# The lanes' turn every four blocks of the receptance and value tiles, in place of every eight

## What is computed

```python
r, k, v, xw, xa, xg = split_cols(rwkv_p, (RWKV_DIM, RWKV_DIM, RWKV_DIM, DECAY_LORA, AAA_LORA, GATE_LORA))
w_log = -jax.nn.softplus(-(rwkv_w0 + jnp.tanh(xw) @ rwkv_w2)) - 0.5
decay = jnp.exp(-jnp.exp(w_log.astype(jnp.float32)))
a = jax.nn.sigmoid(rwkv_a0 + xa @ rwkv_a2)
g = jax.nn.sigmoid(xg) @ rwkv_g2
kk = l2_normalize(hs(k * rwkv_k_k))
k = k * (1.0 + (a - 1.0) * rwkv_k_a)
y = rwkv7_recurrence(r_h, hs(decay), k_h, v_h, -kk, kk * a_h)
y = head_norm(y, rwkv_gn_w, rwkv_gn_b, RWKV_GN_EPS)
bonus = jnp.sum(r_h * k_h * rwkv_r_k, axis=-1, keepdims=True) * v_h
o_rwkv = ((y + bonus.reshape(B, S, RWKV_DIM)) * g).astype(x.dtype)
```

## Time and profile before

| | us |
|---|---|
| median of 3 runs | 3484.59 (3483.98 to 3485.78) |
| the profiled execution, own time | 3487.36 |
| its span, first to last instruction | 3485.6 |
| PE busy in the span | 3373.1 |
| DVE busy in the span | 2252.5 |
| the recurrence with `out_half`'s first tiles, from the trace | 276 (1158 to 1434) |

### The profile page before, as it was taken

How to read it: one execution, slowest core, us unless ns; L and a number is a source line. 1 busy time by engine, 2 the same in 40 slices (tenths; PEclk the granted TensorE clock), 3 DMA queues, 4 the chain that set the end, 5 groups by cost and what they waited for, 6 DMA issues and landing times.

```text
span 3485.6 us, 68747 instructions
## 1 busy us (share of the span) xinstructions
PE 3373.1 (97%) x30086; PEld 3319.7 (95%) x30086; DVE 2252.5 (65%) x3653; ACT 1620.8 (46%) x2339; POOL 56.6 (2%) x78
## 2 busy tenths in 40 slices
PE   7999999999998999999999999998999999999997
PEld 7999999999998888899999999998998999999997
DVE  5656655556676688696666655687546976666455
ACT  5544444444455534364444444464443644444443
POOL 0000000000000000000000000001000000000000
PEclk9999999999999999999999999999999999999998
DMA  6455555555564322255555666542543465555663
GB/s 230 163 176 176 174 176 185 175 180 176 176 197 134 106 89 86 94 171 197 194 194 194 195 191 191 188 151 82 166 147 127 158 199 194 194 194 191 194 198 127
DMA packets 162494, 586.38 MB, mean 168 GB/s; under 512 B 18128, under 2 KB 18128, under 8 KB 161936
## 3 DMA queue, kind: packets, MB, share of 16 engines
q1 hardware_dynamic: 160560, 574.01, 50.4%
q0 software_dynamic: 1632, 7.96, 0.8%
HBM read 579.80 MB, written 2.10 MB: 167 GB/s over the span
## 4 chain that ended last, share of the span: by engine, by line
PE 53%; DVE 8%; ACT 1%; issue 0%; POOL 0%; ACTq 0%; DVEq 0%; POOLq 0%
PE bank L2082 16%; PE bank L2084 16%; PE bank L2083 16%; DVE pairs L2871 2%; PE bank L2295 1%; PE bank L2282 1%; DVE xs L2987 1%; DVE xs L2985 0%; PE bank L2097 0%; PE bank L2099 0%; PE bank L2098 0%; ACT pairs L2548 0%; DVE xr L2955 0%; DVE xr L2875 0%; DVE xs L2901 0%
## 5 line engine op out<-in xcount | busy, mean ns | idle before, releaser
L2082 PE MATMUL bank<-xr,pairs 128*128 128x256 f32 (+1 forms) x5888 | 1660.9, 282 | 35.2 <-DVE pairs L2871 27.3
L2083 PE MATMUL bank<-xr,pairs 128*128 128x256 f32 (+1 forms) x5888 | 1640.3, 279 | 0.0
L2084 PE MATMUL bank<-xr,pairs 128*128 128x256 f32 (+1 forms) x5888 | 1640.2, 279 | 0.0
L2548 ACT ACTIVATE pairs<-raw 128x1024 fp32r<-128x1024 f32 (+1 forms) x1106 | 1143.4, 1043 | 981.3 <-PE bank L2084 791.7
L2871 DVE TENSOR_TENSOR pairs<-raw,pairs 128x1024 fp32r<-128x1024 f32 (+1 forms) x1106 | 1306.3, 1200 | 383.2 <-ACT pairs L2548 380.1
L2082 PEld LDWEIGHTS bank<-xr,pairs 128*128 128x128 f32 x5888 | 1115.7, 189 | 45.9 <-DVE pairs L2871 30.1
L2083 PEld LDWEIGHTS bank<-xr,pairs 128*128 128x128 f32 x5888 | 1113.9, 189 | 1.3
L2084 PEld LDWEIGHTS bank<-xr,pairs 128*128 128x128 f32 x5888 | 1113.3, 189 | 0.0
L2082 PE MATMUL bank<-parts,pairs 128*128 128x256 f32 x1792 | 496.5, 277 | 0.4 <-DVE parts L2875 0.4
L2084 PE MATMUL bank<-parts,pairs 128*128 128x256 f32 x1792 | 495.0, 276 | 0.0
L2083 PE MATMUL bank<-parts,pairs 128*128 128x256 f32 x1792 | 495.0, 276 | 0.0
(11 more groups left out here) (601 smaller groups left out, 3069.3 us busy)
## 6 DMA issues: line engine op xcount, KB each, us to landing
raw<-in_w_in SPq DMA_DIRECT2D x176, 512.0 KB, 4.5
raw<-in_gate SPq DMA_DIRECT2D x176, 512.0 KB, 5.5
raw<-in_val SPq DMA_DIRECT2D x176, 512.0 KB, 4.4
raw<-in_down SPq DMA_DIRECT2D x160, 512.0 KB, 4.4
raw<-in_l_w_in SPq DMA_DIRECT2D x144, 512.0 KB, 4.0
raw<-in_w_out SPq DMA_DIRECT2D x64, 512.0 KB, 4.8
raw<-in_l_w_out SPq DMA_DIRECT2D x64, 512.0 KB, 3.9
raw<-in_v_in SPq DMA_DIRECT2D x48, 512.0 KB, 5.3
```

The lines of the kernel that those rows point to most:

```text
L2082: mm(o, wh[:, q, :], rh[:, k, :], start=begin and q == 0, stop=False)
L2083: mm(o, wh[:, q, :], rl[:, k, :], start=False, stop=False)
L2084: last = mm(o, wl[:, q, :], rh[:, k, :], start=False, stop=end and q == c - 1)
L2548: e.activation(pair_of(n)[0], v3(raw_of(n), widths[n] // slices[n]), ACT.Copy).then_inc(*hi_made(n))
```

## The change

The two calls that issue the column matmuls of the receptance and the value tile pass `step` 4:

```diff
             p2 = v3(j.rv.view, 2)
-            col_tile(p2[:, 0, :], W(16 + c), X2, last.at, j.rv)
-            j.m = col_tile(p2[:, 1, :], W(24 + c), X2, last.at, j.rv)
+            col_tile(p2[:, 0, :], W(16 + c), X2, last.at, j.rv, 4)
+            j.m = col_tile(p2[:, 1, :], W(24 + c), X2, last.at, j.rv, 4)
             j.set = get(sets)
```

## The result

The change made the kernel slower, by more than was forecast:

| | before | after |
|---|---|---|
| median, us | 3484.73 (3483.98 to 3485.78, 4 runs) | 3528.64 (3527.20 to 3530.83, 4 runs) |
| the profiled execution, own time | 3487.36 | 3529.16 |
| its span | 3485.6 | 3527.4 |
| the recurrence, first `lora` matmul to last output matmul (L2397) | 275.3 | 316.6 |
| of it idle on PE, as shown | 11.0 | 29.0 |

A forecast was written before the change was run, and what follows sets the result against it. PE, busy 97% of the span, was taken as the bound. Bursts +8.4, bare stretches -7.8 and late preparation +25.8 sum to +26.4, cut for overlap to +22: 3506.6 us, range 3484 to 3526.

The forecast's parts named there:

- more bursts: Small matmuls among column matmuls: 73 groups in place of 38, each costing PE 0.24 us beyond its work, +8.4 us.
- shorter bare stretches: Two stretches without column matmuls: 20 turns left in place of 32, 3.9 us saved in each, -7.8 us.
- late preparation: At bonus matmul L2327 and at L2362: PE waits for VectorE's preparation, with column-matmul cover halved, +25.8 us.
- discount for overlap: Over the recurrence: VectorE catches up while PE waits, so the summed +26.4 was cut to +22 us.
- clock: Matmuls behind PE's long waits might run at 1.2 GHz, about 1.7 us lost each; left out of the sum.
- A slower PE also shortens the next wait, so I leave it out of the sum: Behind long PE waits: slow matmuls shorten the following wait, so their cost got no term, only a rival.
- rival 3: Behind most long waits the clock falls, six times 1.7 to 2.3 us on top: about +34, 3519 us; 16%.
- I take the middle, +22: Over the recurrence: chosen between the full sum, +26.4, and +18 at the ratio of the first cycle's walk.
- a walk over one cycle: First cycle followed on the clock: +6.0 us, where the terms' share would be 8.7.
- the price of 1.0 us a turn: In the new bare stretches: 20 turns at 1.0 us each, about 20 us a stretch, 5 of them lost.
- Rivals 1 and 2: Better-mixed lanes, bonus waits under about 1 us: 3475 us, 9%; 1.45 us waits cancelling bare-stretch savings: 3485 us, 13%.

The follow-up runs named there:

- value only: Kernel before with four-block turns for the value tile alone, the receptance tile keeping eight; 3494.41 us, ratio 1.0026.
- the filler kernel: Changed kernel with ten filler matmuls on constants between preparation steps PE waits for ahead of the bonus, c = 0, 1, 2, 5, 6; 3524.22 us, ratio 1.0111.
- two turns at once: Changed kernel's number of turns, taken two at a time every eight blocks instead of one every four; 3533.57 us, ratio 1.0138.

## Why the prediction was wrong, and what in it was right

The direction and the mechanism were right; the forecast of 3506.6 was 22 us short, and the time lies 2.6 us above the range. In the predicted order:

| term | predicted | measured | from |
|---|---|---|---|
| more bursts | 35 x 0.24 = +8.4 | some +14, or 0.4 each | what the other rows leave over |
| shorter bare stretches | -7.8 | about -6.2 | 72.8 to 44.3 us, less 22.3 of lane work moved out |
| late preparation | +25.8 | +23.7 | PE's idle time outside the bare stretches, 2.8 to 26.5 |
| discount for overlap | -4.4 | none | |
| clock | left out | +6.2 in column matmuls, some +3 to 4 in small ones | matmuls behind the waits |
| sum | +22 | +41.2 | |

The lane work moved out is an estimate: each matmul at the mean distance between starts that its kind has in the kernel before. The first row is a remainder and holds whatever else is not in the others; value only gave the same 0.4 for a burst.

**The step that failed first is "A slower PE also shortens the next wait, so I leave it out of the sum".** The clock was the largest term that was mis-sized: put at nothing, it measured some 9 to 10 us. It came as rival 3 had it ("falls at most of the long waits"), with 16%. The earlier trace rows had shown it for a wait of 3.06 us, and five of the forecast's own waits were as long or longer. The reason for leaving it out holds in part only: the filler kernel got 4.4 us back net of its own matmuls. The other reason, the bare stretches at 1.00, came from gaps of 1.3 us at most and says nothing of a gap of 3. The Trainium skill (TensorE: Matmul & The Clock Gate, "HAM oscillation — how this bites in real kernels") says that repeated idle time between groups of matmuls costs the clock again and again; the trace agrees, with 0.90 and 0.93 over the stretches with long waits and 1.00 over the bare ones with short ones.

**The second is "I take the middle, +22".** From a walk over one cycle that gave 6.0 for 8.7 I concluded that the terms overlap, and cut a sum of 26.4. The walk held the same assumption as the sum: that PE, once released, runs at full pace. It did not. With the full sum the forecast would have been 3511, which is still 18 short.

**The bursts**: 0.24 us was read where two lanes' steps stand together with 24 column matmuls behind the earlier trace rows. One lane's step with 12 behind costs 0.29 by the rows above, and about 0.4 is left for each over the region, which makes this term 5 to 6 us too small.

**The waits** were walked well one by one, and their mechanism was the predicted one, down to the third mask ahead of L3171. Predicted for c = 0 to 2: 2.1, 4.7, 3.6; measured 2.6, 4.9, 2.9. (The terms written out for c = 1 give 4.5, not 4.7: 1191.9 and 11.8 make 1203.7.) In front of L2362: 3.6 for c = 3, and most of 5.5 for c = 4, where 3.06 and 3.71 were measured; c = 5 2.5 against 3.1, c = 6 3.35 against 2.0. These waits are some 22 us where 25.8 were forecast. The wait of c = 7 (1.45 before), which was to stay, is gone. New was a wait of 2.7 us of `out_half`'s first column matmul (at 1388.92) for a low part, L2875, where before had 0.4 us; the walk did not contain it.

**The bare stretches** came out near the forecast: their idle time fell from 8.2 to 2.5 us, and the price of 1.0 us a turn was close (22.0 and 22.3 us for 20 turns and the burst ahead of them, 1.06 each).

With these put right: 22 + 4.4 (no discount) - 2.1 (waits) + 9.7 (clock) + 1.6 (bare stretches) + 5.6 (bursts, the remainder) = 41.2.

**Rivals 1 and 2** fell at the point that the prediction named: the bonus waits are not under 1 us. The Trainium skill (Perfetto Trace Analysis, "Optimization Strategy") holds that interleaving regimes with different bound engines may gain; the gain was about 6 us here, in the bare stretches, and the costs beside it some 47.

**Still open**: how much of the +41.2 the clock would keep if all waits were filled (the filler covered five lanes of eight, and not L2362); how the remainder of some 14 us divides between the bursts and the pace of small matmuls; and why a turn in a bare stretch costs 1.0 to 1.1 us whatever the mix. An order in which VectorE's low parts give way to a late preparation was not tried.

## What to carry to other kernels

Before making a side stream take turns more often, look up the chain that it starts with, on whatever engines it runs, and ask how many microseconds of the main engine's work lie between its issue and its first use: here 10.8 us stood under 11.3 of cover, and halving it cost 15.5 us of waits directly, and their price in clock on top. Once two chains are late in one in-order queue, putting one ahead of the other moved the wait on, and so did more turns for the later one; more turns for the first gave a third of the loss back; with four-block turns in the value tile alone, the long waits for both were gone. When you price a wait on TensorE, add what the matmuls behind it cost at 1.2 GHz, if any row of the trace shows the clock falling after a wait of such a length.

## What the runs showed of the hardware

- After waits of 2.6 to 4.9 us for the bonus, the next 12 column matmuls took 2.25 to 2.84 us and not 1.57 (granted clock 0.50 behind the longest); after the one of 1.98 us, at c = 6, they took 1.55. With two turns at once, the column matmuls behind a wait of 5.02 us started 0.21 us apart from 1206.13 to 1210.19, and the rest 0.12 apart again.
- A wait of 3.06 us at L2362 had the same effect on the matmuls behind it, in the trace of after: column matmuls from 1274.66 to 1276.80 start 0.21 us apart.
- The same wait cut into gaps of 1.12, 0.90 and 0.20 us by 20 matmuls of 128 columns kept the granted clock at 1.00, and the column matmuls behind took 1.55 us.
- A burst of small fp32 matmuls costs 0.29 us beyond the work in the rows shown: the first large matmul behind it starts late, and the next 0.22 us after it, in place of 0.12 (1436.14 to 1436.36 in the trace of after).
